# A decoder layer with an expert gather: some rows' v summed by ScalarE and GpSimd, and others by VectorE, in place of TensorE

## The reference

```python
def block(xb):
    qh = (xb @ w_q).reshape(tb, PK_HEADS, 2, PK_HALF)
    s = einsum('thpd,hpkd->thpk', qh, sub_keys)
    ...
    ue = jnp.take(u, eidx, axis=0)
    h = gelu(einsum('thkd,td->thk', ue, xb), approximate=False)
    ve = jnp.take(v, eidx, axis=0)
    return einsum('thk,thkd->td', g * h, ve)
x = layer_norm(ALPHA * x + peer(x, ...), ln2_g, ln2_b)
x = x + sigmoid(x @ ple_w_gate) * (p @ ple_w_proj)
```

## Time and profile before

| | us |
|---|---|
| median of 3 runs | 1951.69 |
| lowest, highest | 1951.54, 1954.43 |
| the profiled execution | 1950.47 |
| its span, first to last instruction | 1948.4 |

### The profile page before, as it was taken

One profiled execution on the slowest core, in us unless ns is written; L12 is line 12 of the kernel. 1 busy time (PEld: TensorE's weight loads), 2 busy tenths in 40 slices (PEclk: granted clock), 3 DMA queues, 4 the chain that ended last, 5 costly groups with the idle time before them and its releaser, 6 DMA issues.

```text
span 1948.4 us, 18467 instructions
## 1 busy us (share of the span) xinstructions
PE 1691.0 (87%) x5680; PEld 995.3 (51%) x5680; DVE 1247.0 (64%) x2717; ACT 883.0 (45%) x2075; POOL 493.0 (25%) x530
## 2 busy tenths in 40 slices
PE   8999989869988979899999987788787779887787
PEld 6888767768877646544444532233222224322223
DVE  4454484368986778856556666666666676666643
ACT  6566573134347611535344444454444454444432
POOL 0000000022221212322223333333333333333330
PEclk9999999889999989999999999999999999999998
DMA  5112267699997899999899999999999999999992
GB/s 205 59 50 86 86 238 282 235 385 365 344 330 282 335 363 356 404 413 399 317 337 420 409 416 421 421 379 408 421 418 421 422 404 397 412 421 421 422 415 103
DMA packets 92890, 653.89 MB, mean 336 GB/s; under 512 B 10240, under 2 KB 12800, under 8 KB 14592
## 3 DMA queue, kind: packets, MB, share of 16 engines
q0 software_dynamic: 73728, 536.90, 68.2%
q1 hardware_dynamic: 19072, 115.90, 15.8%
HBM read 650.67 MB, written 2.10 MB: 335 GB/s over the span
## 4 chain that ended last, share of the span: by engine, by line
PE 39%; DMA 25%; ACT 16%; DVE 14%; issue 5%; POOL 0%; SPq 0%; DVEq 0%; ACTq 0%; POOLq 0%
DMA uv<-in_pk_uv,idx 22%; PE psum L1631 17%; DVE uv L1262 6%; PE psum L1599 4%; PE psum L1394 4%; PE psum L1556 4%; PE psum L1659 2%; PE psum L1509 2%; PE psum L1570 2%; ACT diag L805 2%; ACT L793 1%; ACT coef L797 1%; DMA raw<-in_w_branch_a 1%; ACT w_hi L735 1%; DMA raw<-in_w_in 1%
## 5 line engine op out<-in xcount | busy, mean ns | idle before, releaser
L1631 PE MATMUL psum<-uv,diag 128*128 128x512 f32 x1748 | 853.1, 618 | 164.9 <-ACT diag L805 161.5
L1262 DVE CUSTOM_DVE_ANT_0 uv<-uv,psum 128x1024 f32<-128x1024 f32 x512 | 623.7, 1219 | 366.5 <-DMA uv<-in_pk_uv,idx 360.6
L561 POOL DMA_INDIRECT uv<-in_pk_uv,idx x512 | 489.6, 956 | 1412.2 <-PE psum L1631 694.1
L1631 PEld LDWEIGHTS psum<-uv,diag 128*128 128x128 f32 x1748 | 315.7, 193 | 654.2 <-ACT diag L805 373.2
L793 ACT ACTIVATE gelu<-dots 128x1 f32<-128x1 f32 x512 | 103.2, 202 | 726.3 <-DVE dots L1262 724.4
L805 ACT ACTIVATE diag<-ident,coef 128x128 f32<-128x128 f32 x437 | 175.5, 402 | 14.3
L797 ACT ACTIVATE coef<-gelu,weight 128x1 f32<-128x1 f32 x512 | 150.9, 295 | 16.6
L1537 PE MATMUL psum<-xTh,w_hi 128*128 128x384 f32 x320 | 114.8, 359 | 21.2 <-DVE w_lo L1085 21.2
L1394 PE MATMUL psum<-xTh,w_hi 128*128 128x512 f32 x256 | 105.2, 411 | 9.6 <-DVE xTl L984 9.6
L1537 PE MATMUL psum<-xTl,w_hi 128*128 128x384 f32 x320 | 113.1, 353 | 0.0
L1537 PE MATMUL psum<-xTh,w_lo 128*128 128x384 f32 x320 | 112.0, 350 | 0.0
(11 more groups left out here) (205 smaller groups left out, 1947.9 us busy)
## 6 DMA issues: line engine op xcount, KB each, us to landing
raw<-in_w_in SPq DMA_DIRECT2D x56, 1024.0 KB, 6.8
raw<-in_pk_w_q SPq DMA_DIRECT2D x16, 1024.0 KB
raw<-in_w_branch_a SPq DMA_DIRECT2D x8, 1024.0 KB, 8.3
raw<-in_w_branch_b SPq DMA_DIRECT2D x8, 1024.0 KB, 7.1
raw<-in_w_out SPq DMA_DIRECT2D x8, 1024.0 KB, 8.9
uv<-in_pk_uv,idx POOLq DMA_INDIRECT x512
w_gate<-in_ple_w_gate SPq DMA_DIRECT2D x1, 4096.0 KB, 16.7
x_raw<-in_x_t SPq DMA_DIRECT2D x4, 512.0 KB, 7.4
```

The costliest lines, as they stand in the source:

```text
L561: pool.indirect_dma_start(uv[:, r % UV, :], None, pk_uv, bass.IndirectOffsetOnAxis(idx[:, i % 2, j:j + 1], 0)).then_inc(row_in[r % UV], 16)
L1262: V.tensor_tensor_reduce(u, u, x_cur[:], 1.0, 0.0, ALU.mult, ALU.add, dots[:, r % 32:r % 32 + 1]).then_inc(dot_done, 1)
L1631: last = T.matmul(B[i][:], diag[:, n % DR, :], uv[:, r % UV, D + i * 512:D + (i + 1) * 512], start=(r in FIRST), stop=(k == BLOCK_ROWS - 1 ...
```

## The change

Rows are divided among three engines by a table, `summed_by`: P for TensorE as before, V for VectorE as before, G for the new way. In the new way ScalarE multiplies v by coef in place in the ring buffer (128x1024) instead of making a diagonal, and GpSimd adds it to an accumulator of its own (its first row of a block is a copy). GpSimd does the sum of row r - 6 just before it issues the load of row r, in the same queue. The accumulator is `x1T0` in block 0 (its first sum waits for the last query of block 0, which reads `x1T0`) and a new 4 KB tile after. Two small tiles move to make place for it (`qhT1`, `pT`). VectorE's rows now begin anew in each block, and near the end of each block `add_acc(b)` adds each accumulator that the block used into PSUM by two matmuls.

By the table, VectorE has rows in blocks 0 and 1 only, GpSimd in all four. Counts of P, V, G: before 437, 75, 0; after 369, 73, 70.

```diff
+        def summed_by(r):
+            b, k = divmod(r, BLOCK_ROWS)
+            if b == 0:
+                if r < 9:
+                    return "V"
+                if r <= 42:
+                    return "GVGPGVGP"[r % 8]
+                if r <= 60:
+                    return "GVVGVVGP"[r % 8]
+                if r <= OUT_ROW[-1]:
+                    return "GVV"[r % 3]
+                return "PPGPVP"[r % 6] if r <= 120 else "P"
+            if b == 1:
+                return "PVPG"[k % 4] if 4 <= k <= 30 else "PPGPVP"[k % 6] if 30 < k <= 104 else "P"
+            return "PPPG"[k % 4] if 4 <= k <= 30 else "P"
-        SHARED = [r for r in range(OUT_ROW[-1] + 1) if not (9 <= r <= 60 and r % 8 in (2, 5, 7))]
+        SHARED = [r for r in range(ROWS) if summed_by(r) == "V"]
+        POOLED = [r for r in range(ROWS) if summed_by(r) == "G"]
-        ACC_ROW = BLOCK_ROWS - 2
+        ACC_ROW = [BLOCK_ROWS * (b + 1) - 2 for b in range(TB)]
...
+            def sum_v(r):
+                b = r // BLOCK_ROWS
+                n = POOLED.index(r)
+                v = uv[:, r % UV, D:2 * D].rearrange("p (k t) -> p k t", t=P)
+                if n > 0:
+                    pool.wait_ge(pool_step, n)
+                pool.wait_ge(v_scaled, n + 1)
+                if first_of(POOLED, r):
+                    if b == 0:
+                        pool.wait_ge(t_done, USE["query", 0, PKH - 1, 1] + 1)
+                    else:
+                        pool.wait_ge(acc_out, 2 * b)
+                    pool.tensor_copy(acc_pool(b), v).then_inc(pool_step, 1)
+                else:
+                    pool.tensor_tensor(acc_pool(b), acc_pool(b), v, ALU.add).then_inc(pool_step, 1)
             for r in range(ROWS):
+                if r - UV in POOLED:
+                    sum_v(r - UV)
...
+                if r in POOLED:
+                    act.wait_ge(coef_done, r + 1)
+                    nc.scalar.activation(uv[:, r % UV, D:2 * D], uv[:, r % UV, D:2 * D], ACT.Copy,
+                                         scale=coef[:, r % 8:r % 8 + 1]).then_inc(v_scaled, 1)
                     return
...
-                if n == 0:
+                if first_of(SHARED, r):
                     V.tensor_scalar(acc, v, c, None, ALU.mult).then_inc(acc_step, 1)
...
+            def add_acc(b):
+                for sums, rows, step in ((acc, SHARED, acc_step), (acc_pool(b), POOLED, pool_step)):
+                    if not any(r // BLOCK_ROWS == b for r in rows):
+                        continue
+                    pe.wait_ge(step, up_to(rows, b))
+                    for i in range(2):
+                        T.matmul(B[i][:].rearrange("p (k t) -> p k t", t=P), ident[:], sums[:, 4 * i:4 * i + 4, :],
+                                 start=False, stop=False, skip_group_check=True)
```

More of the change, by code:

```diff
@@ L152, in build @@
         uv = place("uv", [UV, 2 * D], F32, o_ring)
-        qhT = [small("qhT0", [2, P]), place("qhT1", [2, SEQ - P], F32, o_mix + 16 * K)]
+        qhT = [small("qhT0", [2, P]), place("qhT1", [2, SEQ - P], F32, o_conv)]
         ln1 = [gaT[:, :, 0:P], gbT[:, :, 0:P]]
@@ L158, in build @@
         ln2 = [ln2_gain[:], ln2_bias[:]]
-        pT = place("pT", [PLE // P, P], F32, o_mix + 19 * K)
+        pT = small("pT", [PLE // P, P])
         x2 = place("x2", [D], F32, o_mix + 20 * K)
@@ L165, in build, with acc_pool @@
         x1T0 = ycT[:, :, 0:P]
+        acc_later = place("acc_later", [KT, P], F32, o_mix + 16 * K)
+        def acc_pool(b):
+            return x1T0 if b == 0 else acc_later[:]
         w3_hi = place("w3_hi", [KT, P], F32R, o_raw + 16 * K)
@@ L237, in build @@
         rec_done, weight_done = sem("rec_done"), sem("weight_done")
-        acc_step = sem("acc_step")
+        acc_step, pool_step, v_scaled = sem("acc_step"), sem("pool_step"), sem("v_scaled")
         acc_out = sem("acc_out")
@@ L275, in build, with up_to, first_of @@
         SEARCH = [(i, search_rows(i)) for i in range(1, ITEMS)]
-        SHARED = [r for r in range(OUT_ROW[-1] + 1) if not (9 <= r <= 60 and r % 8 in (2, 5, 7))]
+        def summed_by(r):
[15 more added lines that the diff above has]
+        POOLED = [r for r in range(ROWS) if summed_by(r) == "G"]
         SHARED_LAG = 2
         JOBS_FIRST = OUT_ROW[-1]
-        ACC_ROW = BLOCK_ROWS - 2
+        ACC_ROW = [BLOCK_ROWS * (b + 1) - 2 for b in range(TB)]
+        def up_to(rows, b):
+            return len([q for q in rows if q < BLOCK_ROWS * (b + 1)])
+        def first_of(rows, r):
+            return r == min(q for q in rows if q // BLOCK_ROWS == r // BLOCK_ROWS)
         def v_count(r):
-            return r + 1 - len([q for q in SHARED if q <= r])
+            return r + 1 - len([q for q in SHARED + POOLED if q <= r])
         def v_reader(r):
@@ L288, in v_reader @@
                 return acc_step, SHARED.index(r) + 1
+            if r in POOLED:
+                return pool_step, POOLED.index(r) + 1
             return v_used, v_count(r)
@@ L799, in row @@
                 if r in SHARED:
+                    return
+                if r in POOLED:
+                    act.wait_ge(coef_done, r + 1)
+                    nc.scalar.activation(uv[:, r % UV, D:2 * D], uv[:, r % UV, D:2 * D], ACT.Copy,
+                                         scale=coef[:, r % 8:r % 8 + 1]).then_inc(v_scaled, 1)
                     return
@@ L1615, in score @@
                     last.then_inc(t_done, 1)
-            FIRST = [min(r for r in range(BLOCK_ROWS * b, BLOCK_ROWS * (b + 1)) if r not in SHARED) for b in range(TB)]
+            FIRST = [min(r for r in range(BLOCK_ROWS * b, BLOCK_ROWS * (b + 1)) if r not in SHARED + POOLED) for b in range(TB)]
             def sum_v(r):
@@ L1741, in _ @@
                     tail_row(r)
-                    if r > 0 and r - 1 not in SHARED:
+                    if r > 0 and r - 1 not in SHARED + POOLED:
                         sum_v(r - 1)
-                if r >= JOBS_FIRST and r not in SHARED:
+                if r >= JOBS_FIRST and r not in SHARED + POOLED:
                     sum_v(r)
-                if r == ACC_ROW:
-                    add_acc()
+                if r in ACC_ROW:
+                    add_acc(ACC_ROW.index(r))
                 if r > JOBS_FIRST:
```

## The result

The changed kernel takes 1995.0 us (median of 4 runs, 1993.9 to 2000.4) against 1951.6 before: the ratio is 1.0227, with a 95% interval from 1.0204 to 1.0249. It is 43 us slower, where 40 us faster was forecast. The profiled execution took 2000.4 us (span 1998.6), 5 us above the median, so its stages add up to somewhat more than 43 us.

What follows compares the result with a forecast made beforehand. PE and VectorE bound rows 9 to 42, PE alone rows 132 to 157, DMA at 421 GB/s from row 200 on. Terms -8 -2 -4 -15 -3.5 -5 -4 +1.5 = -40 us gave 1912 us, range 1890 to 1943.

Steps and rivals of the forecast that it cites:

- GpSimd's add beside VectorE: Rows 9 to 42: add taken as 2.0 us, VectorE meeting some delay, so -8 us instead of about -10.
- ScalarE's scale: Rows 9 to 42: at most +16 us on ScalarE's 59.6 of 146.2, covered; rows 43 to 60: +6 us, stage -2.
- the later release of VectorE's rows: DMA-bound stages: buffers free after 7.5 us against 4.54, priced at nothing; at most 3 us per VectorE row if cover is gone.
- the rule against it: The skill's rule: VectorE instructions with two SBUF inputs and GpSimd instructions reading SBUF exclude each other for their whole length.
- The queue of GpSimd: GpSimd's sums stand ahead of row loads in its queue; the later issue was priced at nothing in DMA-bound stages.
- TensorE's part of rows 9 to 42: Rows 9 to 42: five rows off PE, -9.8 us to 127.9 busy; at 94% busy the stage becomes 136 us.
- Adding the accumulators into PSUM: Block ends: 1.9 us of PE each, five more, hidden where PE idles except the last, +1.5 us on the end.
- Rows 132 to 157: Block 1: PE alone bounds, 13 rows off it give -25.4 us of PE; DMA allows 19.2, taken as -15.
- The ceiling of 421 GB/s: All stages: DMA moves at most 421 GB/s, so a stage's floor is its bytes divided by 421.
- the first rival: Rows 9 to 93: GpSimd's sum stops VectorE for its full length; +4 in rows 9 to 42, total 1929 us; chance 0.2.
- The stages near the ceiling: Gains by missing GB/s: rows 158 to 199 -3.5, 200 to 255 0, heads of blocks 2 and 3 -5 and -4 us.
- Rows 94 to 127: PE relieved by 15.7 us, but 403 GB/s against 421 allows 4.7, so -4 us.

Runs made afterwards that it cites:

- the short add: The changed kernel with GpSimd's add cut to 8 of the 1024 numbers of a row; 1964.5 us, ratio 1.0059.
- port and order out of the way: The changed kernel with GpSimd's add cut to 8 numbers and ScalarE's scale moved behind the row's other work; 1942.3 us, ratio 0.9950.
- the old table of block 0: Kernels with block 0's rows divided as before the change; with blocks 1 to 3 as changed 1947.9 us, other variants 1938.8 to 1951.7 us.
- the two variants of block 1: Old block 0, no GpSimd rows, early accumulator adds, blocks 2 and 3 all TensorE: VectorE in block 1's rows 4 to 104, 1942.1 us; 4 to 30 only, 1938.8.
- the kernel with writes only: The changed kernel with GpSimd's add replaced by two writes of zeros that read nothing; 1966.6 us, ratio 1.0080.
- the kernel with the early add and the scale last: The changed kernel with full GpSimd adds, ScalarE's scale after the row's other work, accumulators added into PSUM earlier; 1966.6 us, ratio 1.0087.

## Why the prediction was wrong

Two steps carry the miss: GpSimd's add beside VectorE, priced at next to nothing, and ScalarE's scale, called covered. A third, the later release of VectorE's rows, is seen in a trace but was not tested.

**GpSimd's add beside VectorE** failed as a choice. The forecast set the cost to VectorE aside ("some delay") and kept the rule against it as a rival with a chance of 0.2, because no row of the trace before showed such a pair. The mechanism of that rival is what happened. But its price was wrong too: it counted VectorE's load against the length of the stage (116 + 34 us of 146.2) and got +4. VectorE was not a pool of work to be filled up to the stage's length. In rows 9 to 60 PE waits for VectorE's part of the split, which waits for ScalarE's, which stands behind the gelu of a row and so waits for the dot. A stop of VectorE is then a stop of the stage: 28.0 us more busy time, 24.2 us more stage. The earlier trace rows showed this chain, with VectorE's part waiting 28.9 us for ScalarE's and PE 11.0 us for VectorE's in 84 us, and the forecast used it for rows 43 to 60 only. The other place of that rival, rows 83 to 93 with +2.9, showed nothing: 33.6 us against 34.0.

**ScalarE's scale** was priced by ScalarE's busy share ("covered") in rows 9 to 42; rows 43 to 60 were charged for it, but with the whole stage still at -2. It cost 23 to 25 us over the 24 GpSimd rows of both, about 1 us each. The term that was needed is the interval of two dots in a row that has a weight split: 1.22 + gelu and coefficient + scale + 1.05 + 1.22. All of its terms but the scale were in the trace, and the scale had a row of like size. The scale itself took 1.15 us where 1.05 was used.

**The queue of GpSimd** was priced at nothing, rightly as far as tested: two writes of 2.13 us in its place cost nothing beyond the short add in rows 9 to 60 (242.5 against 242.8 us).

**TensorE's part of rows 9 to 42** was right under its own condition: with port and order out of the way, rows 9 to 42 take 136.5 us with PE busy 127.6 of them, where the forecast worked out 136 and 127.9. Rows 9 to 60 together take 9.9 us less than before, where it had 8 and 2.

**Adding the accumulators into PSUM** was priced at nothing but for the end, +1.5. The wait of VectorE behind it was missed: row 129 comes 1.7 us later after its forerunner than before, and row 257 2.6 us. Moved forward it gave 5 to 7 us back in one kernel and 6 to 7 in another (by the ratios and by the medians). The end itself did not move: from row 511's dot to the end 35.6 us against 35.5.

**Rows 132 to 157** held: -13.8 us in the changed kernel, -15 forecast, and -13 to -19 in the experiments. The ceiling of 421 GB/s held as well; none of the stages of the earlier trace rows in blocks 1 to 3 moved more than that in any kernel.

**The signs.** The split at 1.71 us on average is the sign of the first rival. TensorE's clock below 0.9 in block 1, named as a sign of being wrong, came too (0.88 in rows 200 to 255) but is not what cost the time there: the stage took 144.0 us against 142.2, with the DMA busy all of it.

**The stages near the ceiling** did not give what their missing GB/s allowed. Rows 158 to 199 took 115.7 us in the changed kernel and 110.3 to 112.5 us in the kernels with the old table of block 0, against 108.7 before. Their bytes rose from 44.0 to between 44.9 and 45.4 MB, 2 to 3 us at the ceiling: part of the gain of the stage before is paid there. What moves into the stage is bytes of the rows' own loads (41.2 to 42.3 and 42.7 MB on GpSimd's DMA queue in the two kernels looked at), not weight loads (2.75 MB in each). The heads of blocks 2 and 3 gained nothing from TensorE's relief: without it they took 106.4 and 105.7 us before and 105.9 to 108.1 in two experiments, with VectorE's rows 108.7 to 111.6, and with GpSimd's 106.5 to 111.5.

**Rows 94 to 127** were forecast at -4, by TensorE's relief and the ceiling, and came out at +7.3. That is neither the add nor the scale's place: without the add they take 119.0 us, with the scale last as well 120.3, and with the old table of block 0 110.2 to 113.4. Among what the table adds there are VectorE's sums, two rows late, whose later release the forecast priced at nothing. This is the one of row 106 in the changed kernel:

```profile
887.38 1.22 DVE L1317 CUSTOM_DVE_ANT_0 uv<-uv,psum 128x1024 f32<-128x1024 f32 x1 [12.57 <-DMA uv<-in_pk_uv,idx]
...
893.50 1.28 DVE L1330 SCALAR_TENSOR_TENSOR oT<-uv,coef,oT 128x1024 f32<-128x1024 f32 x1
...
895.55 0.94 POOL L611 DMA_INDIRECT uv<-in_pk_uv,idx  x1 [12.34 <-DVE oT L1330]
```

The load into the freed buffer is issued 8.2 us after the dot, where the forecast had 7.5 for a VectorE row and 4.54 for a TensorE row. The forecast took that as covered by the loads that are queued; here the dot had itself waited 12.57 us for its load, so there was no cover. In all, loads wait 20.2 us for VectorE's sums in rows 104 to 127, where in the kernel before VectorE has no sum. That this is the cause of the +7.3 is not shown.

**Open.** No run changed rows 94 to 127 alone. Their first ten, 94 to 103, took 39.7 us with the short add and the scale last against 35.8 before; the table gives VectorE two sums and GpSimd one row there, beside the three norms. The last 3 us between the two variants of block 1 stay below what was resolved.

## What to carry to other kernels

Price work that is moved to an idle engine by the chain it lands in, not by the share of that engine: in an in-order engine an instruction put ahead of one that the critical path waits for can cost its full length each time (here about 1 us of 1.15 in each of 24 rows), and some places later in the same row nothing. Before GpSimd gets elementwise work that reads SBUF, count VectorE's instructions with two SBUF inputs as stopped while it runs, above all where another engine waits for them. The full length of every add is the upper end: 24 GpSimd rows of 2.37 us are 57 us in rows 9 to 60, and VectorE became 28 us busier. And look at when a buffer is released: a sum that waits for a later row's dot waits for whatever that dot waits for. Last, look at where an accumulator is folded in: right before the last step of a stage it is on the path of whoever waits for that step.

## What the hardware showed beyond the forecast

A float32 add of 128x1024 on GpSimd takes 2.34 to 2.41 us in the changed kernel, a copy of the same size 1.04 us, a memset of it in the kernel with writes only 0.96 to 0.97 us. Small VectorE instructions are stopped as well, of the scalar kind too: the 128x16 subtraction that takes 0.22 us at the median and 0.44 at most before took up to 2.84 us in the changed kernel. The dots, with one input in PSUM, were not: 54 of them overlap an add, and their median is the 1.22 us of the others (one took 2.66). VectorE's multiply-add of 128x1024 into its accumulator, with two SBUF inputs, was hardly touched (1284 ns on average against 1281 in the earlier trace rows): it follows the dot at once, while the add waits for the scale, and so only one of the 71 overlaps an add at all. That one took 1.62 us and ended 1.09 us after the add, as the splits do.

To start first did not protect an instruction. The longest split, 4.00 us, starts at 453.25, 0.54 us before the add beside it (453.78 to 456.15), and it too ends 1.09 us after the add; two more splits start 0.38 and 0.45 us ahead and end the same way. In the kernel with the early add and the scale last, one add took 3.39 us, 1.0 more than the others, where a VectorE instruction with two SBUF inputs had started 0.10 us before it. What decides which of the two waits is not shown.
